# A gMLP and channel-MLP layer in fp32: the MLP's input moved by four transfers per block within SBUF, with its tokens held by fours

## The chip, the core and the metric

The kernel runs on one core of a Trainium2 chip. The metric is the device time of one execution, in microseconds (us), as the median of several runs. One further execution was recorded by the hardware profiler; all rows below come from it.

## What is computed

One layer over `x` of 1024 tokens by 1024 features, all in fp32. With `DEPTH` 1 only the first mixer, the gMLP, is used:

```python
hn = rms_norm(x, norm1_g)
z = gelu(hn @ w_in)                      # 1024 x 4096
u, v = split(z)
v = layernorm(v) * ln_g
sv = einsum('gts,bnsge->bntge', ws, v) + b_s      # causal ws, chunks of 128 tokens
x = x + (u * sv) @ w_out                 # 2048 -> 1024; the result is called y below
x = x + square(relu(rms_norm(x, norm2_g) @ w1)) @ w2   # 1024 -> 4096 -> 1024
return rms_norm(x, final_g)
```

## The kernel before

**Products.** The large matrix products are cut into products of 1024x1024 by 1024x1024, and each of these is done by a Strassen scheme: seven products of 512x512 blocks in place of eight. The code calls the left-hand blocks `a11`, `a12`, `a21`, `a22` and their sums `s1` to `s4`, the right-hand ones `b..` with sums `t..`, and the results `c11`, `c12`, `c21`, `c22`. Every fp32 operand is split into a high part (rounded to fp32r, ScalarE, ACT in the rows) and a low part (the rest, VectorE, DVE in the rows), and TensorE (PE) does three products for each: high by high, high by low, low by high (L438, L442, L443, function `products`).

**Stages.** A *single* (`single(n)`, n = 0 to 7) is one such 1024-deep product: n = 0, 1 make v, n = 2, 3 make u, n = 4 to 7 make the MLP's hidden layer. A *double* (`double(d)`) goes over 2048 of depth: d = 0 is the product with `w_out`, d = 1, 2 are those with `w2`. The order is singles 0 to 3, double 0, singles 4 to 7, doubles 1 and 2. Each has seven positions (`pos`), one per block product. A position has four units in a single and eight in a double, a unit being twelve matmuls of 128x512; below "unit (pos, k)" is the k-th of a position. The right operand of a unit is split into a ring of four entries (`ring_high`, `ring_low`; for doubles `pair_high`, `pair_low`, which hold both operands): ACT refills an entry when PE has left it (`split_high`, `split_pair_high`), DVE follows with the low part (`split_low`, `split_pair_low`), and PE waits for it before the unit (`low_done`). All engines run lists in program order, written out by hand; only semaphores join them. DVE also does the sums of the weights (`sum_t`), adds the finished banks of PSUM into `rows` (`add_rows` for doubles, `add_block` for singles), and SyncE (SP) issues nearly every transfer, on one queue.

**From double 0 to single 4.** y leaves double 0 in four blocks of 512 tokens by 512 features, held in `rows`, in the order c12, c22, c11, c21 (`Y_FINAL`: after positions 3, 4, 5, 6). Single 4 needs y transposed, as its left operand, so each block goes into a tile `quad_a..` by DMA, is turned by DVE's 32x32 transposes (`turn_y`, four instructions per block, into `raw_a..`), scaled by the norm's gain, and split. c12 becomes a11, c22 a21, c11 a12, c21 a22. Then come s3 from a21 and a11, s2 from a22 and s3 (`sum_turned`), s1 from s2 and a11 (`sum_combo`), and s4. Single 4 takes its left operands in the order a11 (pos 0), a12 (1), s2 (2), s1 (3), s3 (4), s4 (5), a22 (6).

How a block reaches its `quad` tile before the change:

- c12 and c22: SP stores the block to DRAM (`y_of`), waits for it to land, and loads it back by four transfers (`load_quads`, L808), one for each quarter of 32 partitions.
- c11: sixteen transfers within SBUF, all issued by SP (`move_quads`, L396), each of 32 partitions by 4 pieces of 512 bytes.
- c21: the same sixteen, eight issued by SP and eight by ACT.

Every block is also stored to DRAM, since double 1 needs y again as the residual (`load_rows`). The scheme holds token 128m + p on partition p of slice m; the reciprocal mean squares of y (`y_r2`), one per token, are computed at the start of double 1 and multiply PE's result in `add_rows`.

Of the kernel before, what the change touches and what calls it, by code (L numbers as in the profile page):

```python
# [10 lines left out]
P = 128  # L11
T = 1024
D = 1024
# [103 lines left out]
def trunk(nc, x, norm1_g, norm2_g, mlp_w1, mlp_w2, final_g, a_w_in, a_ln_g, a_ws, a_bs, a_w_out, out):  # L117
    x_v = x.rearrange("a (m p) d -> p (a m) d", p=P)
    out_v = out.rearrange("a (m p) d -> p (a m) d", p=P)
# [6 lines left out]
    with ExitStack() as ctx:  # L126
# [103 lines left out]
        y_r2 = tiny("y_r2", [P, MT])  # L230
        o_sq = tiny("o_sq", [P, 2, MT])
# [11 lines left out]
        scale_dram = nc.dram_tensor("row_scales", [MT, P], F32).ap()  # L243
        y_dram = nc.dram_tensor("y_blocks", [4, NB, NB], F32).ap()
# [6 lines left out]

        def y_of(blk):
            return y_dram[BLOCKS.index(blk)].rearrange("(k p) s -> p k s", p=P)

        def y_quadrant(blk, q):

            return y_dram[BLOCKS.index(blk)].rearrange("(t r) (q c) -> q r t c", r=32, q=4)[q]
# [78 lines left out]
        y_step = sem("y_step")  # L336
        o_squared = sem("o_squared")
# [299 lines left out]
        def _(sp):  # L637
# [87 lines left out]
            def single(n):  # L725
# [23 lines left out]
                if n in (3, 7):  # L749
                    filled(sp, ("product", n, 2), set_of(slot(n, 2))[3])  # L750
                    load_pair(0 if n == 3 else 1, "b11")
                if kind(n) == "v" or kind(n) == "hid":
# [30 lines left out]
                if kind(n) != "u":  # L783
                    store_block(n, "c22")
                if n not in (3, 7):
# [12 lines left out]
            def load_rows(d, blk):  # L798
# [3 lines left out]
                      "c22": x_v[:, 4:8, NB:]}[blk] if d == 0 else y_of(blk), rows_landed[blk], f"rows_{blk}")  # L802

            def load_quads(b, blk, dst):

                sp.wait_ge(y_stored[blk], 16)
                for q in range(4):
                    sp.dma_start(dst[32 * q:32 * q + 32, :, :], y_quadrant(blk, q)).then_inc(quads_landed[b], 16)  # L808

            def double(d):  # L810
# [90 lines left out]
                if d == 0:  # L901
                    y_final(sp, "c22")
# [1143 lines left out]
```

## Time and profile before

| | |
|---|---|
| median of 3 runs | 1123.8 us (1123.45 to 1123.99) |
| the profiled execution | 1123.38 us |
| its span | 1121.3 us |
| around the span | 2.1 us |
| PE busy | 1110.0 us, 99% |
| DVE busy | 796.9 us, 71% |
| ACT busy | 563.3 us, 50% |
| granted PE clock | 0.999 of full speed |
| DMA queue q1 | 49.6% of 16 engines, 194.28 MB |

The span goes from the first to the last record of the program. PE is busy nearly all of it, so what the kernel could still lose lies in PE's few gaps. Idle time of the other engines costs nothing unless PE waits for them.

### The profile page before, as it was taken

How to read it: one execution, taken by the hardware profiler on the slowest of the kernel's cores; microseconds unless marked ns; L12 is line 12 of the kernel's file. 1: busy time of each engine (PE TensorE's matmuls, PEld its weight loads, DVE VectorE, ACT ScalarE, POOL GpSimd, SP SyncE). 2: the span in 40 equal slices, each digit the busy share in tenths (PEclk: the TensorE clock that was granted, in tenths of full speed). 3: DMA queues.
4: the chain of work that ended last, by engine and by line, in shares of the span. 5: the costliest groups of instructions: out<-in, count | busy, mean ns of one | idle time of the engine just before them, and what ended most of it. 6: DMA issues, size and time to landing. Idle time of an engine off the chain costs nothing.

```text
span 1121.3 us, 13104 instructions
## 1 busy us (share of the span) xinstructions
PE 1110.0 (99%) x5050; PEld 922.8 (82%) x5050; DVE 796.9 (71%) x872; ACT 563.3 (50%) x870; POOL 23.0 (2%) x17
## 2 busy tenths in 40 slices
PE   9999999999999999999999999999999999999997
PEld 7888888888888888888788888888888888888886
DVE  5885656689779986699858447455598575677666
ACT  7764344554554434644674455454644333333456
POOL 0000000000000000000000000000000000000240
PEclk9999999999999999999999999999999999999999
DMA  9072353272875594643353635527878354343213
GB/s 333 16 222 106 107 181 109 93 256 81 319 256 196 186 351 153 191 122 103 114 187 144 194 113 191 196 102 272 301 292 298 121 217 188 113 151 113 78 73 150
DMA packets 86541, 195.90 MB, mean 175 GB/s; under 512 B 5048, under 2 KB 15312, under 8 KB 79824
## 3 DMA queue, kind: packets, MB, share of 16 engines
q1 hardware_dynamic: 85168, 194.28, 49.6%
q10 hardware_dynamic: 1312, 0.79, 0.3%
q8 instruction: 40, 0.66, 0.2%
q14 instruction: 21, 0.17, 0.0%
HBM read 134.23 MB, written 58.72 MB: 172 GB/s over the span
## 4 chain that ended last, share of the span: by engine, by line
PE 89%; DVE 7%; ACT 2%; issue 1%; DMA 1%; SPq 0%; DVEq 0%; ACTq 0%
PE banks L438 29%; PE banks L443 29%; PE banks L442 29%; PE banks L531 3%; DVE ring_low L1426 1%; DVE raw_a L1522 1%; DVE left_and_right L1462 1%; DMA left_and_right<-in_a_w_in_dram 1%; ACT ring_high L990 0%; DVE rows L1589 0%; DVE rows L1568 0%; ACT raw_a L1039 0%; DVE s_low L1512 0%; DVE raw_s L1555 0%; DVE pair_low L1434 0%
## 5 line engine op out<-in xcount | busy, mean ns | idle before, releaser
L1020 ACT ACTIVATE pair_high<-left_and_right 128x1024 fp32r<-128x1024 f32 x168 | 177.2, 1060 | 247.4 <-PE banks L438 199.5
L1426 DVE TENSOR_TENSOR ring_low<-left_and_right,ring_high 128x512 fp32r<-128x512 f32 x224 | 153.1, 693 | 186.0 <-ACT ring_high L990 185.3
L1434 DVE TENSOR_TENSOR pair_low<-left_and_right,pair_high 128x1024 fp32r<-128x1024 f32 x168 | 204.3, 1231 | 111.2 <-ACT pair_high L1020 111.2
L990 ACT ACTIVATE ring_high<-left_and_right 128x512 fp32r<-128x512 f32 x224 | 138.0, 628 | 254.6 <-PE banks L438 155.9
L438 PE MATMUL banks<-pair_high 128*128 128x512 f32 x672 | 262.0, 390 | 0.0
L442 PE MATMUL banks<-pair_low,pair_high 128*128 128x512 f32 x672 | 261.7, 389 | 0.0
L443 PE MATMUL banks<-pair_high,pair_low 128*128 128x512 f32 x672 | 261.7, 389 | 0.0
L438 PE MATMUL banks<-s_high,ring_high 128*128 128x512 f32 x384 | 150.0, 391 | 2.9 <-DVE s_low L1512 2.1
L442 PE MATMUL banks<-s_low,ring_high 128*128 128x512 f32 x384 | 149.6, 390 | 0.0
L443 PE MATMUL banks<-s_high,ring_low 128*128 128x512 f32 x384 | 149.5, 389 | 0.0
L438 PEld LDWEIGHTS banks<-pair_high 128*128 128x128 f32 x672 | 126.2, 188 | 26.4 <-DVE scratch L1616 0.3
L442 PEld LDWEIGHTS banks<-pair_low,pair_high 128*128 128x128 f32 x672 | 126.2, 188 | 26.2
L443 PEld LDWEIGHTS banks<-pair_high,pair_low 128*128 128x128 f32 x672 | 126.2, 188 | 26.0
L438 PE MATMUL banks<-a_high,ring_high 128*128 128x512 f32 x288 | 112.6, 391 | 0.0
L442 PE MATMUL banks<-a_low,ring_high 128*128 128x512 f32 x288 | 112.2, 390 | 0.0
L443 PE MATMUL banks<-a_high,ring_low 128*128 128x512 f32 x288 | 112.2, 389 | 0.0
L438 PEld LDWEIGHTS banks<-s_high,ring_high 128*128 128x128 f32 x384 | 72.1, 188 | 18.8 <-DVE s_low L1512 2.5
L443 PEld LDWEIGHTS banks<-s_high,ring_low 128*128 128x128 f32 x384 | 72.1, 188 | 14.9
L442 PEld LDWEIGHTS banks<-s_low,ring_high 128*128 128x128 f32 x384 | 72.1, 188 | 14.8
L1462 DVE TENSOR_TENSOR left_and_right<-left_and_right 128x2048 f32<-128x2048 f32 x32 | 73.2, 2288 | 1.0
L438 PEld LDWEIGHTS banks<-a_high,ring_high 128*128 128x128 f32 x288 | 54.1, 188 | 11.3 <-DVE scratch L1616 0.3
L443 PEld LDWEIGHTS banks<-a_high,ring_low 128*128 128x128 f32 x288 | 54.1, 188 | 11.2
(128 smaller groups left out, 1217.6 us busy)
## 6 DMA issues: line engine op xcount, KB each, us to landing
left_and_right<-sums SPq DMA_DIRECT2D x40, 1024.0 KB, 7.0
left_and_right<-in_mlp_w_dram SPq DMA_DIRECT2D x36, 1024.0 KB, 7.4
sums<-rows SPq DMA_DIRECT2D x34, 1024.0 KB, 5.3
left_and_right<-in_a_w_in_dram SPq DMA_DIRECT2D x19, 1024.0 KB, 7.3
v_blocks<-rows SPq DMA_DIRECT2D x8, 1024.0 KB, 4.5
left_and_right<-in_a_w_out_dram SPq DMA_DIRECT2D x8, 1024.0 KB, 10.0
rows<-in_x_dram SPq DMA_DIRECT2D x7, 1024.0 KB, 9.1
spare<-v_blocks SPq DMA_DIRECT2D x6, 1024.0 KB, 6.6
```

The costliest lines, as they stand in the source:

```text
L438: first = nc.tensor.matmul(ps[:, bank, :], stat_high, mov_high, start=start, stop=False, skip_group_check=True)
L442: nc.tensor.matmul(ps[:, bank, :], stat_high, mov_low, start=False, stop=False, skip_group_check=True)
L443: last = nc.tensor.matmul(ps[:, bank, :], stat_low, mov_high, start=False, stop=stop, skip_group_check=True)
L531: mm = nc.tensor.matmul(ps[:, banks[m], c * P:(c + 1) * P], held[:, c, m * P:(m + 1) * P], ws_t[:, g, :], start=True, stop=True)
L990: nc.scalar.activation(ring_high[k][:, :], right_place(n, pos)[:, k, :], ACT.Copy)\
L1020: nc.scalar.activation(pair_high[pair_entry(d, pos, k)][:, :, :], pair_of(d, pos, k), ACT.Copy)\
L1426: nc.vector.tensor_tensor(ring_low[k][:, :], right_place(n, pos)[:, k, :], ring_high[k][:, :].bitcast(F32), ALU.subtract).then_inc(low_don ...
L1434: nc.vector.tensor_tensor(pair_low[e][:, :, :], pair_of(d, pos, k), pair_high[e][:, :, :].bitcast(F32), ALU.subtract).then_inc(low_done, 1)
L1462: nc.vector.tensor_tensor(*args, ALU.subtract).then_inc(t_summed, 1)
L1522: nc.vector.transpose(dst[:, j, :], src[:, :, j:P:4]).then_inc(y_turned, 1)
```

## The change

**Transfers.** `move_quads` now issues four transfers for a block instead of sixteen: each takes all 128 partitions of one quarter of the features, and writes 32 partitions by 16 pieces of 512 bytes. All four blocks go this way, from SP alone; the way over DRAM is gone for c12 and c22, and ACT issues no transfer there. The store to DRAM follows behind the four transfers. For c22 the load of the last left block of double 0, `left(13)`, still stands ahead in SP's list.

**Token order.** Because of the new shape, column 128m + p of the transposed block is token 4p + m. The hidden layer and the result hold their tokens in that order; so the residual is loaded by `y_fours`, the output is written by a changed `out_v` (rows of 4 KB that lie 16 KB apart in DRAM, instead of side by side), and the scales `y_r2` must be rearranged: they are computed in single 6 (`scale_y`), stored to DRAM and loaded back as `y_r2_fours` in single 7, both by SP. DVE waits for that load before double 1's first `add_rows`.

**DVE's order.** The turns of a11 move up by a position, to between the splits for the start of position 5; the additions of c22 and c11 move to the end of the position before, ahead of the split of k = 3; the turns of a21 move from position 6 to the middle of position 5, those of a12 from the end to the middle of position 6, and a12's low parts to ahead of the first split of single 4. ACT's scaling of a11 and the high parts of a12 move likewise.

```diff
-        def move_quads(eng, b, blk, dst, quadrants):
-            for q in quadrants:
-                for r in range(4):
-                    eng.dma_start(dst[32 * q:32 * q + 32, r:4 * QT:4, :],
-                                  block_of[blk][32 * r:32 * r + 32, :, P * q:P * q + P]).then_inc(quads_landed[b], 16)
+        def move_quads(eng, b, blk, dst):
+            for q in range(4):
+                eng.dma_start(dst[32 * q:32 * q + 32, :, :], block_of[blk][:, :, P * q:P * q + P])\
+                  .then_inc(quads_landed[b], 16)
...
                 if d == 0:
                     y_final(sp, "c12")
+                    move_quads(sp, "a11", "c12", quad_a11)
                     sp.dma_start(y_of("c12"), block_of["c12"]).then_inc(y_stored["c12"], 16)
                 left(11)
-                if d == 0:
-                    load_quads("a11", "c12", quad_a11)
                 left(12)
...
                     y_final(sp, "c22")
+                    move_quads(sp, "a21", "c22", quad_a21)
                     sp.dma_start(y_of("c22"), block_of["c22"]).then_inc(y_stored["c22"], 16)
-                    load_quads("a21", "c22", quad_a21)
...
-                    move_quads(sp, "a22", "c21", quad_a22, (0, 1))
-                    sp.wait_ge(quads_landed["a22"], 256)
+                    move_quads(sp, "a22", "c21", quad_a22)
...
                 elif n == 4:
-                    high_turned("a12")
                     split_high(4, 1, 0)
-                    y_final(act, "c21")
-                    act.wait_ge(low_done, unit_double(0, 6, 7) + 1)
-                    move_quads(act, "a22", "c21", quad_a22, (2, 3))
                     split_high(4, 1, 1)
...
+                    early = d == 0 and pos > 4
+                    if not late and not early:
                         add_rows(d, pos - 1)
-                    if d == 0 and pos == 5:
-                        turn_y("a11")
-                    if d == 0 and pos == 6:
-                        turn_y("a21")
+                        low_a11(4, 0)
...
+                        if d == 0 and pos == 5 and k == 5:
+                            turn_y("a21", [0, 1])
+                        if d == 0 and pos == 5 and k == 6:
+                            turn_y("a21", [2, 3])
+                        if d == 0 and pos == 5 and k == 7:
+                            sum_turned("s3", [0, 1])
+                        if d == 0 and pos == 6 and k == 5:
+                            turn_y("a12", [0, 1])
+                        if d == 0 and pos == 6 and k == 6:
+                            turn_y("a12", [2, 3])
...
                     for k in range(4):
+                        if d == 0 and pos in (4, 5) and k == 3:
+                            add_rows(0, pos)
...
+                            if d == 0 and pos == 4:
+                                turn_y("a11", [k])
+                            if (d, pos, k) == (0, 5, 0):
+                                sum_turned("s3", [2, 3])
```

The order of DVE around the end of position 4 of double 0. `pair_low` is the low part of a unit's operands, `rows` the addition of a finished block of y, `raw_a11` and `raw_a21` are the turned blocks. Before, the split of unit (5, 3), then the additions and the turns of a11:

```order
L1434 TENSOR_TENSOR pair_low0_92<-left_and_right_77,pair_high0_87 128x1024
L1434 TENSOR_TENSOR pair_low1_93<-left_and_right_77,pair_high1_88 128x1024
L1589 TENSOR_TENSOR rows_78<-banks,rows_78 128x512 x4
L1522 STREAM_TRANSPOSE raw_a11_63<-quad_a11_71 128x512 x4
L1434 TENSOR_TENSOR pair_low2_94<-left_and_right_77,pair_high2_89 128x1024
L1434 TENSOR_TENSOR pair_low3_95<-left_and_right_77,pair_high3_90 128x1024
```

Now, from the split of unit (5, 2) on:

```order
L1437 TENSOR_TENSOR pair_low0_92<-left_and_right_77,pair_high0_87 128x1024
L1525 STREAM_TRANSPOSE raw_a11_63<-quad_a11_71 128x512
L1592 TENSOR_TENSOR rows_78<-banks,rows_78 128x512 x4
L1437 TENSOR_TENSOR pair_low1_93<-left_and_right_77,pair_high1_88 128x1024
L1525 STREAM_TRANSPOSE raw_a11_63<-quad_a11_71 128x512
L1437 TENSOR_TENSOR pair_low2_94<-left_and_right_77,pair_high2_89 128x1024
L1437 TENSOR_TENSOR pair_low3_95<-left_and_right_77,pair_high3_90 128x1024
L1525 STREAM_TRANSPOSE raw_a21_64<-quad_a21_72 128x512 x2
L1437 TENSOR_TENSOR pair_low0_92<-left_and_right_77,pair_high0_87 128x1024
L1525 STREAM_TRANSPOSE raw_a21_64<-quad_a21_72 128x512 x2
L1437 TENSOR_TENSOR pair_low1_93<-left_and_right_77,pair_high1_88 128x1024
```

A turn and the four additions have moved ahead of the split of unit (5, 3) (`pair_low1`), and the turns of a21 stand ahead of the splits of units (5, 6) and (5, 7), where none stood.

SP's list over the same stretch and on to single 4. Before:

```order
L887 DMA y_blocks<-rows_78 128x4x512
L644 DMA left_and_right_77<-sums 128x2048
L808 DMA quad_a11_71<-y_blocks 32x16x128 x4
L644 DMA left_and_right_77<-sums 128x2048 x2
L903 DMA y_blocks<-rows_78 128x4x512
L808 DMA quad_a21_72<-y_blocks 32x16x128 x4
L396 DMA quad_a12_73<-rows_78 32x4x128 x16
L908 DMA y_blocks<-rows_78 128x4x512
L644 DMA left_and_right_77<-in_mlp_w1_dram 128x4x512 x2
L396 DMA quad_a22_74<-rows_78 32x4x128 x8
```

Now:

```order
L398 DMA quad_a11_71<-rows_78 32x16x128 x4
L894 DMA y_blocks<-rows_78 128x4x512
L646 DMA left_and_right_77<-sums 128x2048 x3
L398 DMA quad_a21_72<-rows_78 32x16x128 x4
L909 DMA y_blocks<-rows_78 128x4x512
L398 DMA quad_a12_73<-rows_78 32x16x128 x4
L913 DMA y_blocks<-rows_78 128x4x512
L646 DMA left_and_right_77<-in_mlp_w1_dram 128x4x512 x2
L398 DMA quad_a22_74<-rows_78 32x16x128 x4
```

The two round trips over DRAM are gone, the third of the `sums` loads (`left(13)`) stays ahead of a21's move, and every block is moved by four transfers.

## Rows read from the trace of the kernel before

**Rows 1.** The page: busy us, share of the span, instructions.
```profile
PE 1110.0 (99%) x5050; PEld 922.8 (82%) x5050; DVE 796.9 (71%) x872; ACT 563.3 (50%) x870; POOL 23.0 (2%) x17
```

**Rows 2.** Waits of PE, 440:600: waited for, us in total, times, longest.
```profile
PE banks L438 <- DVE s_low L1512: 2.1, 1, 2.1
PE banks L438 <- DVE ring_low L1426: 0.7, 2, 0.4
```

**Rows 3.** Timeline of PE: start us, us, engine line, operands, [idle before <-releaser].
```profile
458.65 0.39 PE L438 MATMUL banks<-pair_high 128*128 128x512 f32 x1
...
502.17 0.39 PE L438 MATMUL banks<-a_high,ring_high 128*128 128x512 f32 x1
...
523.93 0.39 PE L438 MATMUL banks<-s_high,ring_high 128*128 128x512 f32 x1
...
538.35 0.50 PE L438 MATMUL banks<-s_high,ring_high 128*128 128x512 f32 x1 [2.12 <-DVE s_low L1512]
...
541.20 0.39 PE L438 MATMUL banks<-s_high,ring_high 128*128 128x512 f32 x1
```

**Rows 4.** Timeline of DVE, from the end of position 4 to single 4.
```profile
460.02 1.22 DVE L1434 TENSOR_TENSOR pair_low<-left_and_right,pair_high 128x1024 fp32r<-128x1024 f32 x1 [1.27 <-ACT pair_high L1020]
461.17 2.48 DVE L1589 TENSOR_TENSOR rows<-banks,rows 128x512 f32<-128x512 f32 x4
463.56 4.05 DVE L1522 STREAM_TRANSPOSE raw_a<-quad_a 128x512 f32<-128x512 f32 x4
...
507.50 2.75 DVE L1500 SCALAR_TENSOR_TENSOR a_low<-raw_a,g_fours,a_high 128x512 fp32r<-128x512 f32 x4
...
513.58 1.10 DVE L1522 STREAM_TRANSPOSE raw_a<-quad_a 128x512 f32<-128x512 f32 x1
...
536.00 2.29 DVE L1512 TENSOR_TENSOR s_low<-raw_s,s_high 128x2048 fp32r<-128x2048 f32 x1
```

**Rows 5.** DVE in 440:565 by shape: count, busy us, mean ns, idle before.
```profile
L1434 DVE TENSOR_TENSOR pair_low<-left_and_right,pair_high 128x1024 fp32r<-128x1024 f32 x20 | 23.9, 1217 | 11.6 <-ACT pair_high L1020 11.6
L1426 DVE TENSOR_TENSOR ring_low<-left_and_right,ring_high 128x512 fp32r<-128x512 f32 x25 | 16.9, 688 | 6.8 <-ACT ring_high L990 6.6
L1522 DVE STREAM_TRANSPOSE raw_a<-quad_a 128x512 f32<-128x512 f32 x16 | 16.7, 1076 | 0.0
L1555 DVE SCALAR_TENSOR_TENSOR raw_s<-raw_a,neg_g,raw_a 128x512 f32<-128x512 f32 x4 | 2.8, 746 | 0.0
```

**Rows 6.** Timeline of the queues of SP and ACT; the time is that of issuing.
```profile
461.27 0.34 SPq L644 DMA_DIRECT2D left_and_right<-sums  x1
463.74 0.37 SPq L903 DMA_DIRECT2D y_blocks<-rows  x1
468.75 1.91 SPq L808 DMA_DIRECT2D quad_a<-y_blocks  x4
485.49 10.42 SPq L396 DMA_DIRECT2D quad_a<-rows  x16
...
506.58 5.50 ACTq L396 DMA_DIRECT2D quad_a<-rows  x8
```

**Rows 7.** DMA by issue: KB each, median us from issue to landing.
```profile
left_and_right<-sums SPq DMA_DIRECT2D x1, 1024.0 KB, 4.8
...
quad_a<-rows SPq DMA_DIRECT2D x16, 64.0 KB, 2.0
```

**Rows 8.** Busy time by stretch; the last two: share of 16 DMA engines, GB/s.
```profile
466.00:468.00 2.00, 2.00 (x11) 1.65 (x10) 2.00 (x3) 1.86 (x4) 0.00 (x0) 1.00 1.03 402
470.00:474.00 4.00, 4.00 (x19) 3.34 (x18) 0.98 (x1) 4.00 (x12) 0.00 (x0) 1.00 1.09 230
471.00:474.00 3.00, 3.00 (x15) 2.50 (x14) 0.00 (x0) 3.00 (x10) 0.00 (x0) 1.00 1.13 209
508.00:513.00 5.00, 5.00 (x23) 4.14 (x23) 5.00 (x7) 0.80 (x2) 0.00 (x0) 1.00 0.88 200
```

**Rows 9.** Tile row_scales: from issue to landing of the scales' two transfers.
```profile
DMA to landing us min/median/max: 9.4/11.6/13.8
```

More of the change, by code:

```diff
@@ L801, in load_rows @@
                      {"c11": x_v[:, 0:4, 0:NB], "c12": x_v[:, 0:4, NB:], "c21": x_v[:, 4:8, 0:NB],
[L802 to L808, printed above, removed]
+                      "c22": x_v[:, 4:8, NB:]}[blk] if d == 0 else y_fours(blk), rows_landed[blk], f"rows_{blk}")
             def double(d):
@@ L902, in double @@
                     y_final(sp, "c22")
+                    move_quads(sp, "a21", "c22", quad_a21)
                     sp.dma_start(y_of("c22"), block_of["c22"]).then_inc(y_stored["c22"], 16)
-                    load_quads("a21", "c22", quad_a21)
                     sp.wait_ge(low_done, unit_double(0, 5, 7) + 1)
                     y_final(sp, "c11")
-                    move_quads(sp, "a12", "c11", quad_a12, range(4))
+                    move_quads(sp, "a12", "c11", quad_a12)
                     sp.dma_start(y_of("c11"), block_of["c11"]).then_inc(y_stored["c11"], 16)
@@ L1305, in double @@
                         square_rows(2, "c11", o_sq, o_squared, (0, 1))
+                    if pos == 5 and d == 0:
+                        scale_a11()
                     split_pair_high(d, pos, 5)
+                    if pos == 5 and d == 0:
+                        high_a11()
                     if pos == 6 and d == 2:
@@ L1312, in double @@
                         square_rows(d, "c12", y_sq if d == 0 else o_sq, y_squared if d == 0 else o_squared)
+                    split_pair_high(d, pos, 6)
+                    if pos == 5 and d == 2:
+                        square_rows(2, "c22", o_sq, o_squared)
+                    split_pair_high(d, pos, 7)
                     if pos == 5 and d == 0:
-                        scale_a11()
-                    split_pair_high(d, pos, 6)
-                    if pos == 5 and d == 0:
-                        high_a11()
-                    if pos == 5 and d != 1:
-                        square_rows(d, "c22", y_sq if d == 0 else o_sq, y_squared if d == 0 else o_squared)
-                    split_pair_high(d, pos, 7)
+                        square_rows(0, "c22", y_sq, y_squared)
                     if pos == 6 and d == 0:
                         square_rows(0, "c11", y_sq, y_squared)
+                        high_turned("a12")
                     for k in range(4):
@@ L1384, in _ @@
             act.wait_ge(o_done_b, MT)
-            act.dma_start(out_v[:, 7, NB:], rows[:, 7, NB:]).then_inc(last_stored, 16)
+            act.dma_start(out_v[1, :, 3, NB:], rows[:, 7, NB:]).then_inc(last_stored, 16)
         @block.vector
@@ L1518, in turn_y @@
                             "a22": (quad_a22, raw_a22)}[blk]
-                dve.wait_ge(quads_landed[blk], 64 if blk in ("a11", "a21") else 256)
+                dve.wait_ge(quads_landed[blk], 64)
                 dve.wait_ge(low_done, unit_double(0, 3 if blk == "a12" else 4, 7) + 1)
@@ L1695, in single @@
                 elif n == 4:
-                    low_turned("a12")
                     split_low(4, 1, 0)
@@ L1699, in single @@
                     split_low(4, 1, 1)
-                    for k in range(2):
-                        turn_y("a22", [k])
-                        sum_turned("s2", [k])
+                    turn_y("a22", [0])
+                    sum_turned("s2", [0])
                     split_low(4, 1, 2)
+                    turn_y("a22", [1])
+                    sum_turned("s2", [1])
                     split_low(4, 1, 3)
```

60 lines of the change are left out of this document (37 added, 23 removed).

## The prediction

> **What bounds the kernel now.** The page comes first: PE is busy 99% of the span [rows 1]. It does the same matmuls before and after, so the change can give back only gaps of PE. The waits of PE come next: in the stretch around the turn from double 0 to single 4 there are three, 2.1 us on a low part of a sum (L1512) and 0.7 us in two pieces on the ring's low parts [rows 2]. The timeline of PE gives what they cost in all. Units follow one another every 2.72 us: the first of position 5 starts at 458.65 and the first of single 4, sixteen units later, at 502.17 [rows 3]. From 523.93 (single 4, position 2) to 541.20 are five units, which should take 13.6 us and take 17.27. So 3.67 us are lost, idle time and slow restarts together, and that is **all that this change can win**: 0.33% of the time.
>
> Why PE waits there is to be seen on DVE. Its chain runs without a break from the first turn of a22, at 513.58, to the end of s1's low part, 536.00 + 2.29 = 538.29 [rows 4]: 24.7 us of work in a fixed order, and PE starts on s1 (position 3) at 538.35 [rows 3]. Without stalls PE would be due there at 502.17 + 12 x 2.72 = 534.8. So s1 is in time if a22's first turn starts by about 510.0, less the 0.1 us or so from DVE's end to PE's start. It starts at 513.58 because the block's sixteen transfers take that long: ACT is busy issuing its eight for 5.50 us from 506.58 on, SP with the other eight beside it [rows 6].
>
> **The price on which all hangs: S, the time for one block (1 MiB) as four transfers.** The trace has no such transfer. Nearest is the load of c22's quads from DRAM, with the same four destinations of 32 partitions and the same 512-byte pieces: it moves 230 GB/s over 470 to 474 and 209 over 471 to 474, the engines' share being above 1 [rows 8]. 1.049 MB at these rates takes 4.6 and 5.0 us. The old moves within SBUF go at 200 GB/s at a share of 0.88, held back by their issue [rows 8]: 5.2 us, my upper end by rows. The lower end is the store of a block in 2 KB pieces over all partitions, 402 GB/s [rows 8]: 2.6 us. I take **S = 4.8**, since the pieces and the destination are those of the quads' load; the source differs (SBUF, not DRAM). To this comes the way to the first packet and the landing of the last: a 64 KB move lands 2.0 us after its issue [rows 7], 0.3 of it its own bytes, so a whole block alone lands 1.7 + S = 6.5 us after the first issue.
>
> The Trainium skill (SBUF — State Buffer, Door 1: The DMA port swizzle) speaks against a fast move: partitions 0 to 31, or any 32 that start at a multiple of 32, reach only 8 of 16 ports, about 218 GB/s, so a transfer that writes one quarter of the partitions is held to half the rate. By that S would be 4.8, where the bare 402 GB/s of the store would make it 2.6. The rates of the quads' load, 209 to 230 GB/s, agree with it, although they come from DRAM.
>
> **Part 1, a11 (c12).** The move starts at once instead of after a store and its landing. a11's turns go into DVE's gaps: 11.6 us of idle time stand before the 20 splits in this stretch [rows 5]. Worth nothing by itself, since PE does not wait here. The load of `left(11)` comes behind 1 MiB more of moves, some 5 us later; it is first read for unit (5, 4), due at 469.5, and issued near 445.
>
> **Part 2, a21 (c22): a new wait.** Before, the split of (5, 3) ends at 460.02 + 1.22 = 461.2, and SP issues `left(13)` at 461.27, since that load waits for it [rows 4, 6]. Now a turn and four additions stand ahead: the split of (5, 2) ends at 458.75, then 1.0 for the turn, 2.4 for the additions and 1.1 for the split (the steps of these groups in rows 4 and 5, where back-to-back instructions overlap by 0.09), so 463.3 (458.75 is 460.02 less the idle 1.27). `left(13)` goes out 2.0 us later, and a21's move queues behind it on the same queue. The load lands 4.8 us after its issue [rows 7]; its packets free the queue some 0.7 earlier, at 463.3 + 4.05 = 467.35. Then S, then 0.35 to land: **472.5**. DVE has come to the turns of a21 some 5 us earlier and stands there, with the split of (5, 6) queued behind two turns. That split ends at 472.5 + 2.0 + 1.2 = 475.7; PE is due on (5, 6) at 458.65 + 6 x 2.72 = 474.97 [rows 3] and starts 0.15 after DVE's end: **0.9 us of stall**. The next unit costs DVE two turns and a split, 3.1 us, against PE's 2.72: **0.4** more.
>
> **Part 3, a12 (c11).** From 472.5 DVE is full: four turns (4.0), five splits of pairs (5.7), four pieces of s3 (2.6) and the four additions (2.4), 14.8 in all with their joins [rows 4, 5]. c11 is final at 487.3, its move lands at 487.3 + 1.7 + 4.8 = 493.8. Meanwhile DVE does 5.1 us of other work and idles a little. From 493.8 come four turns (4.0), two pair splits (2.3), a12's low parts (2.6), two ring splits (1.2) and the additions of c21 (2.4): c21 is final at **506.3**. Single 4's first unit is due at 502.17 plus the 1.3 already lost and its first ring split ends at 503.4: **0.1**.
>
> **Part 4, a22 (c21).** Its move lands at 506.3 + 6.5 = **512.8**, only 0.7 us sooner than before, though ACT no longer issues. The 24.7 us chain then ends at 537.6. PE, by now 1.4 us later and with some 0.2 us of slow restarts, is due on s1 at 534.8 + 1.6 = 536.4 and starts at 537.8: **1.4 us**. The two small waits on the ring go, as PE's lateness covers them.
>
> **Part 5, the rest, at nothing.** The scales' two transfers land in 9.4 and 13.8 us by the like of single 0 [rows 9]; the second is issued in position 6 of single 7, and double 1's first additions come after a whole position of eight units, 22 us, so DVE's wait finds it landed. The output's rows of 4 KB now lie 16 KB apart; the pieces are as long as before, and I bound this by 0.3 us either way. ACT's moved work has gaps around it.
>
> **Sum.** Stalls after: 0.9 + 0.4 + 0.1 + 1.4 = 2.8, and 0.25 for restarts, 3.1 against 3.67 now. The gain is 0.6 us: 1123.4 - 0.6 = 1122.8 for an execution like the profiled one, which lies 0.4 under the median of 1123.8. So **1123.2 us**. As the three moves a21, a12, a22 stand one behind the other, with DVE full between them, each 0.1 us in S is 0.3 in the time. S of 4.56 gives 1122.4, 5.24 gives 1124.5.
>
> **The rivals.** 2.25 us (0.2%) is about what a measurement can tell from no change.
>
> *All stalls gone.* SBUF as source gives the engines shorter packets than DRAM, and S is at most 4.2. Then a21's turns start by 471.9, PE loses 0.7 there at the most, and s1 is in time. For it: the store's 402 GB/s shows that the engines can do more, and the engines' share of 0.88 at 200 GB/s leaves room for 227 [rows 8]. Against it: the share above 1 at 209 GB/s, which looks like a limit at the destination. Time: 1120.3 to 1121.5, or 1120.1 at best.
>
> *The moves are slow and the stalls grow.* One mechanism: each transfer reads 128 partitions and writes 32, all sixteen engines crowd on the same 32, and S is 5.75 or more. From there the time is over 2.25 us worse. At S = 6 the first stall is 2.1, splits (6, 6) and (6, 7) stall by 0.8, (4, 0, 0) by 0.5, and all three old waits are back with 3.1: with restarts 6.9 against 3.67, 1127.0 us. For it: a new shape that nothing in the trace shows, and DVE blocked in order behind each landing. Against it: the same destination pattern at 4.6 to 5.0.
>
> *The change does nothing for a22.* If c21's move were bound by issue as before, it would land where it did, and the new stalls at (5, 6) would be pure loss, hidden in part by s1's old wait: 1123.5 to 1124.5, the same for a measurement. It is in my middle case.
>
> **How the numbers follow.** The middle case, S from 4.3 to 5.7, has 0.60, and its own range is 1121.6 to 1125.5. All stalls gone has 0.26, slow moves 0.14. The range reaches down to the best case, 1120.1, and up to S of 5.6 with the 0.3 us of the output, 1125.9. Faster by over 0.2%: 0.26; within: 0.60; slower: 0.14.
>
> **What would show it.** In the changed kernel's timeline of DVE the first turn of a21 should start near 472.5, that of a12 near 493.8, of a22 near 512.8, each after an idle time ended by a DMA; PE should show new waits on `pair_low` in position 5, about 1.3 us together, and one on `s_low` of about 1.2. The rate over 468 to 472 should be 210 to 230 GB/s. If it is above 250, or the turns of a21 start before 471.9, the middle case is wrong towards faster; if the rate is below 185, towards slower. A wait of DVE for the scales, or a gap in PE anywhere outside 470 to 540, would mean that I missed something.

## The result, and the profile after

The change makes the kernel slower. Four runs of the changed kernel have a median of 1139.9 us (1139.1 to 1140.6), the kernel before beside them 1123.9. The ratio is 1.0143, with a 95% interval of 1.0124 to 1.0163. Forecast were 1123.2 us and a range up to 1125.9, so the time lies 14 us above the range. (One run of the kernel before took 1396 us in a disturbed execution; the ratio leaves it out.)

The page's first part, where [rows 1] stood:

```profile
span 1138.7 us, 13083 instructions
PE 1115.4 (98%) x5050; PEld 924.4 (81%) x5050; DVE 796.8 (70%) x872; ACT 564.0 (50%) x870; POOL 23.0 (2%) x17
```

The span is 17.4 us longer, with as many matmuls and the same work on DVE and ACT. PE's own busy time is 5.4 us longer, although it does the same matmuls; the granted clock below accounts for most of that. The waits of PE and of DVE over 440 to 600, against [rows 2]:

```profile
PE banks L440 <- DVE pair_low L1437: 9.3, 2, 7.0
PE banks L440 <- DVE ring_low L1429: 2.6, 4, 0.7
PE banks L440 <- DVE s_low L1515: 2.1, 1, 2.1
```

```profile
DVE raw_a L1525 <- DMA quad_a<-rows: 24.6, 3, 11.3
```

The wait on the sum's low part is as long as before. New is a wait on the pairs' low parts, 7.0 us at once, and above it DVE's: three times, 24.6 us in all, it stands before the turns of a block until the block's transfers have landed. Each is seen in the timelines of SP, with the issue of the moves, and of DVE, with the turns (the transposes of `raw_a`; in brackets the idle time before):

```profile
463.32 3.10 SPq L398 DMA_DIRECT2D quad_a<-rows  x4
...
493.28 2.71 SPq L398 DMA_DIRECT2D quad_a<-rows  x4
...
517.75 2.77 SPq L398 DMA_DIRECT2D quad_a<-rows  x4
```

```profile
478.45 2.04 DVE L1525 STREAM_TRANSPOSE raw_a<-quad_a 128x512 f32<-128x512 f32 x2 [11.31 <-DMA quad_a<-rows]
...
505.09 2.05 DVE L1525 STREAM_TRANSPOSE raw_a<-quad_a 128x512 f32<-128x512 f32 x2 [6.09 <-DMA quad_a<-rows]
...
529.40 1.09 DVE L1525 STREAM_TRANSPOSE raw_a<-quad_a 128x512 f32<-128x512 f32 x1 [7.20 <-DMA quad_a<-rows]
```

From a block's first issue to its first turn it takes 11.8 us for a12 (493.28 to 505.09) and 11.65 for a22 (517.75 to 529.40); for a21 it takes 15.1, since `left(13)` goes ahead of it. The prediction had 6.5. The stretches of time say the same as a rate; the columns are start and end, length, busy time of PE, PEld, DVE, ACT and POOL, then TensorE's granted clock, the share of the DMA engines and GB/s:

```profile
470.00:474.00 4.00, 4.00 (x19) 3.34 (x18) 0.00 (x0) 4.00 (x10) 0.00 (x0) 1.00 1.27 119
474.00:478.00 4.00, 0.67 (x3) 0.21 (x2) 0.00 (x0) 0.32 (x1) 0.00 (x0) 1.00 1.16 199
478.00:482.00 4.00, 0.34 (x1) 0.34 (x2) 3.55 (x4) 0.00 (x0) 0.00 (x0) 0.70 0.34 130
482.00:486.00 4.00, 4.00 (x10) 3.12 (x10) 4.00 (x6) 1.06 (x1) 0.00 (x0) 0.50 0.00 0
```

From 470 to 474 only the moves are under way (the store of the block, in its 2 KB pieces, comes behind them and lifts the next stretch): 119 GB/s, with the engines' share at 1.27, where the quads' load had 230 [rows 8]. So the DMA engines are not idle; it is their packets that take long.

The last column but two, the granted clock, tells most of PE's longer busy time. After the pause of 7 us the clock is granted at 0.50 (1.2 GHz), and from the second start on PE's timeline shows steps of 0.43 us instead of 0.23:

```profile
474.28 0.39 PE L445 MATMUL banks<-pair_high,pair_low 128*128 128x512 f32 x1
481.66 0.79 PE L440 MATMUL banks<-pair_high 128*128 128x512 f32 x1 [6.99 <-DVE pair_low L1437]
482.25 0.63 PE L444 MATMUL banks<-pair_low,pair_high 128*128 128x512 f32 x1
482.68 0.63 PE L445 MATMUL banks<-pair_high,pair_low 128*128 128x512 f32 x1
```

Adding up each gap between two starts beyond 0.227 us over 440 to 584 gives 3.6 us for the kernel before and 21.2 for the changed one. The difference, 17.6, is the 17.4 of the span to within 0.2. 2.3 us are slow steps after the first pause, 1.6 slow steps after the wait for s1 at 551.6; the rest is waiting.

### The profile page after: what moved, and what is told of

Same layout as the page of the kernel before. It is cut to its first block, busy times and chain, and to the rows that moved or that the text cites. A ratio compares the mean times of both kernels' runs of the same rounds, so it can differ in the third digit from the quotient of the medians.

```text
span 1138.7 us, 13083 instructions
## 1 busy us (share of the span) xinstructions
PE 1115.4 (98%) x5050; PEld 924.4 (81%) x5050; DVE 796.8 (70%) x872; ACT 564.0 (50%) x870; POOL 23.0 (2%) x17
## 4 chain that ended last, share of the span: by engine, by line
PE 86%; DVE 6%; DMA 3%; issue 2%; ACT 2%; SPq 1%; DVEq 0%; POOL 0%; ACTq 0%; POOLq 0%
PE banks L440 28%; PE banks L445 28%; PE banks L444 28%; DMA quad_a<-rows 3%; PE banks L533 3%; DVE ring_low L1429 1%; DVE raw_a L1525 1%; DVE left_and_right L1465 1%; DVE pair_low L1437 1%; DVE rows L1592 1%; SPq L398 1%; ACT ring_high L994 0%; DVE raw_s L1558 0%; DVE rows L1571 0%; DVE s_low L1515 0%
## 5 line engine op out<-in xcount | busy, mean ns | idle before, releaser
L440 PEld LDWEIGHTS banks<-pair_high 128*128 128x128 f32 x672 | 126.7, 188 | 37.2 <-DVE pair_low L1437 10.7
L445 PEld LDWEIGHTS banks<-s_high,ring_low 128*128 128x128 f32 x384 | 72.4, 188 | 15.1
```

Source lines behind the costliest of these rows:

```text
L440: first = nc.tensor.matmul(ps[:, bank, :], stat_high, mov_high, start=start, stop=False, skip_group_check=True)
L445: last = nc.tensor.matmul(ps[:, bank, :], stat_low, mov_high, start=False, stop=stop, skip_group_check=True)
```

## Is it the time of the moves? Sixteen transfers again, on one queue and on two

Two theories stood against each other. *Time of the move*: DVE's order puts three moves in series, and each is some 5 us longer than forecast. *Order*: the new order of DVE costs the 16 us, whatever the transfers take. Both runs keep DVE's order and the token order of the change, and move each block in sixteen pieces of 64 KB to the same places. Each piece reads every fourth partition, 32 in all, so size and number of partitions read change together here; the measurements further below take them apart.

```diff
             for q in range(4):
-                eng.dma_start(dst[32 * q:32 * q + 32, :, :], block_of[blk][:, :, P * q:P * q + P])\
-                  .then_inc(quads_landed[b], 16)
+                for r in range(4):
+                    eng.dma_start(dst[32 * q:32 * q + 32, 4 * r:4 * r + 4, :],
+                                  block_of[blk][r:P:4, :, P * q:P * q + P]).then_inc(quads_landed[b], 16)
```

On SP alone:

> The change as it is, but each block moved by sixteen transfers of 64 KB (32 partitions to 32) from SyncE's queue alone, to the same places. Before, sixteen such took 10.42 us to issue and landed 2.0 us after their issue, so a block takes 12.4 us from the first issue, against 2.8 + 8.3 = 11.1 with the four transfers. Theory time of the move (the three moves in series, nothing else): 1.3 us more in each of three, 1139.9 + 3.9 = 1143.8. Theory order (VectorE's new order costs the 16 us, whatever the transfers take): 1139 to 1141.

Measured: 1139.06 us (1137.9 to 1139.9), ratio 1.0127 (1.0110 to 1.0144). That is the number of the *order* theory, and the expectation of the other one missed by 4.7 us. The trace tells why. The first turns wait for a DMA here as well:

```profile
476.20 2.04 DVE L1526 STREAM_TRANSPOSE raw_a<-quad_a 128x512 f32<-128x512 f32 x2 [8.74 <-DMA quad_a<-rows]
502.96 2.04 DVE L1526 STREAM_TRANSPOSE raw_a<-quad_a 128x512 f32<-128x512 f32 x2 [6.20 <-DMA quad_a<-rows]
528.38 1.08 DVE L1526 STREAM_TRANSPOSE raw_a<-quad_a 128x512 f32<-128x512 f32 x1 [8.32 <-DMA quad_a<-rows]
```

a21 is turned 2.2 us earlier than with the four, since the sixteen are issued while `left(13)` is still under way, which hides a part of their issue. a12's move then takes 11.9 us from its first issue (491.04) and a22's 12.8 (515.59), 0.1 and 1.1 more than the four. The three together make 1.0 us, and the time is 0.8 us shorter than the changed kernel's. Three equal losses were wrongly expected, and this run by itself does not tell the theories apart.

With half of the transfers of a21, a12 and a22 issued by ACT:

```diff
-                    move_quads(sp, "a21", "c22", quad_a21)
+                    move_quads(sp, "a21", "c22", quad_a21, (0, 1))
+                    sp.wait_ge(quads_landed["a21"], 256)
...
                     if pos == 5 and d == 0:
+                        y_final(act, "c22")
+                        move_quads(act, "a21", "c22", quad_a21, (2, 3))
                         scale_a11()
```

> As the one before, but eight of the sixteen transfers of the last three blocks are issued by ScalarE, at the places where it has just split a half. 5.2 to 5.5 us of issue and 2.0 us to land give about 7.4 us from the first issue, where the prediction had taken 6.5 and the changed kernel takes 11.1. Theory time of the move: 3.7 us less in each of three, 1139.9 - 11.1 = 1128.8, or 1123.2 + 3 x 0.9 = 1125.9 counted from the prediction; so 1125 to 1130. Theory order: stays at 1138 to 1141.

Measured: 1127.09 us (1126.0 to 1130.1), ratio 1.0020 (1.0010 to 1.0030) against a kernel before that had 1125.5 beside it. That lies in the 1125 to 1130 of *time of the move*. Over 12 us are gone without a touch on DVE's order, which the *order* theory can't have. The turns of a21 start at 472.94, and those of a12 wait for no transfer:

```profile
472.94 2.11 DVE L1538 STREAM_TRANSPOSE raw_a<-quad_a 128x512 f32<-128x512 f32 x2 [0.48 <-DMA quad_a<-rows]
...
495.67 2.09 DVE L1538 STREAM_TRANSPOSE raw_a<-quad_a 128x512 f32<-128x512 f32 x2
...
517.34 1.10 DVE L1538 STREAM_TRANSPOSE raw_a<-quad_a 128x512 f32<-128x512 f32 x1 [0.26 <-DMA quad_a<-rows]
```

472.94 is what was forecast for the four transfers (472.5), and still this kernel is no faster than the one before. One reason is the price of ACT's help. Eight issues hold it for 5.7 us, the scaling of a11 and the next split stand behind them, and DVE's split of the next unit, ahead of the turns, waits 6.22 us for it (the last row). The other reason is PE's wait on s1, which is as long as before; more of it below.

```profile
461.89 5.69 ACTq L399 DMA_DIRECT2D quad_a<-rows  x8
467.69 2.56 ACT L1061 ACTIVATE raw_a<-raw_a,g_fours 128x512 f32<-128x512 f32 x4 [5.10 <-issue]
...
471.23 1.23 DVE L1450 TENSOR_TENSOR pair_low<-left_and_right,pair_high 128x1024 fp32r<-128x1024 f32 x1 [6.22 <-ACT pair_high L1028]
```

## Are the moves in series? One block alone, and the old order

First, of the changed kernel a21's move alone goes by sixteen transfers over the two queues, with a12 and a22 as they are.

> The change as it is, but c22's move into a21 alone by sixteen transfers of 64 KB, eight each on SyncE's and ScalarE's queue, as in the run with all three; a12 and a22 by four. There a21's first turn began at 472.9, with the change at 478.5. Theory series: 5.5 us less, 1139.9 - 5.5 = 1134.4, and the first turns of a12 and a22 come 5.5 earlier as a whole. Theory that the last move alone sets the end (a22 is what s1 waits for): unchanged near 1139.

Measured: 1134.06 us (1133.0 to 1134.7), ratio 1.0079 (1.0062 to 1.0095). The first turns of the three blocks:

```profile
473.69 2.10 DVE L1535 STREAM_TRANSPOSE raw_a<-quad_a 128x512 f32<-128x512 f32 x2 [1.01 <-DMA quad_a<-rows]
...
499.79 2.04 DVE L1535 STREAM_TRANSPOSE raw_a<-quad_a 128x512 f32<-128x512 f32 x2 [5.50 <-DMA quad_a<-rows]
...
524.02 1.08 DVE L1535 STREAM_TRANSPOSE raw_a<-quad_a 128x512 f32<-128x512 f32 x1 [6.68 <-DMA quad_a<-rows]
```

They come 4.8, 5.3 and 5.4 us earlier than in the changed kernel, and the time falls by 5.8, where 5.5 were expected. What one move saves is handed on whole through the two others. They are in series.

Then the reverse: all four moves by four transfers, with the new token order and the scales over DRAM, but DVE's and ACT's order as it was before the change (of its diff only a part is shown).

```diff
-                        if d == 0 and pos == 5 and k == 5:
-                            turn_y("a21", [0, 1])
-                        if d == 0 and pos == 5 and k == 6:
-                            turn_y("a21", [2, 3])
...
+                    if d == 0 and pos == 5:
+                        turn_y("a11")
+                    if d == 0 and pos == 6:
+                        turn_y("a21")
```

> The change's four transfers for all four blocks, with the tokens by fours and the scales through HBM, but VectorE's and ScalarE's order as before: a11 and a21 turned late, ahead of positions 5 and 6 of the double, a12's low parts in single 4. Only two moves are then waited for at once. a12: 485.5 + 11.7 = 497.2, before its turns of 498.8, so nothing. a22: 506.6 + 11.65 = 518.2 where the first turn started at 513.6, so 4.6 us. Theory series (the loss is the move's time, as often as VectorE's order waits for it): 1123.8 + 4.6 = 1128.4, that is 11.5 less than with the new order, because a21's and a12's moves have slack again. Theory moves alone (the slow transfers cost the same under any order): 1137 or more. Theory order alone (the new order costs the 16 us): 1123.5 to 1124.5.

Measured: 1129.16 us (1127.8 to 1129.8), ratio 1.0036 (1.0024 to 1.0048) with 1124.4 for the kernel before beside it, so 4.8 us over it by the medians and 4.0 by the ratio, where 4.6 were expected. Of all the turns only the first of a22 waits; the turns of a12, the first row, do not:

```profile
498.69 2.09 DVE L1523 STREAM_TRANSPOSE raw_a<-quad_a 128x512 f32<-128x512 f32 x2
...
518.07 1.08 DVE L1523 STREAM_TRANSPOSE raw_a<-quad_a 128x512 f32<-128x512 f32 x1 [4.49 <-DMA quad_a<-rows]
```

The same slow transfers cost 4 to 5 us under the old order and 16 under the new one. The old order turns a21 some 20 us after its block is final and so does not feel that move. In this trace the gaps of PE over 440 to 584 add up to 9.7 us, 6.1 more than before, and the span is 6.1 us longer: nothing is left for the token order, the scales and the output's rows. (3.1 of the 9.7 are slow steps at 1.2 GHz after the pauses at 518 and 540; not every execution need have them, and the medians differ by less.)

## What makes a block slow: the transfers by themselves

Four kernels compute nothing, but move one block of 1 MiB in one form after the other, with no engine at work beside it.

> Nothing of the reference is computed; the output is x read back. One block of 1 MiB lies in SBUF as in the kernel (128 partitions, 4 x 512 elements in each) and is moved by fourteen forms, one after the other, each landed before the next is issued. In the changed kernel a block's four transfers (each reads 128 partitions and writes 32) land one every 2.27 us. Theory shape (a transfer that reads 128 partitions and writes only 32 within SBUF is slow by itself): here too about 2.3 us for each of the four, 9 us a block; straight to the same partitions in pieces of 512 bytes well below, 5 us or less; 32 partitions to 32 others in the same pieces under 5 us; 128 to 32 in pieces of 2 KB as slow as in 512 bytes. Theory load (the transfers are slow because three engines and TensorE use SBUF at the same time): all forms near 5 us here. Theory pieces (a move within SBUF in pieces of 512 bytes costs about 80 ns a piece in any shape): every form with 512-byte pieces near 9 us, the one with 2 KB pieces near 5, and from HBM to the same places 5. The sixteen transfers of 64 KB are held up by their issue, 10.4 us, in every theory.

What SyncE waited for after the last issue of a form (in all, times, longest):

```profile
SPq L55 <- DMA four_fourths<-rows: 8.6, 1, 8.6
SPq L55 <- DMA wide_pieces<-rows: 7.6, 1, 7.6
...
SPq L55 <- DMA from_dram<-blocks: 4.6, 1, 4.6
...
SPq L55 <- DMA straight<-rows: 2.7, 1, 2.7
```

With the 2.7 us of issue the four transfers of the change (`four_fourths`) take 11.3 us here too. So it is not the load of the other engines. It is not the piece either: in 2 KB pieces (`wide_pieces`) it is 10.2 with the issue. From HBM to the same 32 partitions it is 7.2, within SBUF to the same 128 partitions 5.4. The sixteen transfers of 64 KB on one queue take 11.7 and 11.9 us, 10.3 and 10.4 of them issue.

> Nothing of the reference is computed; the output is x read back. As in the first measurement a block of 1 MiB is moved by one form after the other, nothing else running; this time the number of partitions read and written is varied, all in pieces of 512 bytes that do not merge. Known: 128 to 32 lands 11.3 us after its first issue (packets of 82 ns), HBM to 32 in 7.2 (38 ns), 32 to 128 in 8.0 (39 ns), 128 to the same 128 in 5.4 (28 ns). Theory both sides (a transfer within SBUF is held by the narrower side, and writing 32 partitions while reading costs twice): 32 to 32, of the same partitions or others, as slow as 128 to 32, 11 us. Theory spread (slow is that each DMA engine reads eight partitions and writes two, the ratio of read to written partitions being four): 128 to 64 and 64 to 32 in between, 8 to 9 us, 64 to 64 and 32 to 32 near 6 to 7.5 us. Theory queue (a transfer alone takes 47 ns a packet, queued behind others 82): two, landed, then two takes 2 x (0.65 + 1.7 + 4.5) = 13 us or less and its packets are at 50 to 60 ns. Over two queues, the sixteen of 64 KB should land 7.4 us after the first issue, the eight of 128 KB from 64 partitions in 2.7 + 2.3 = 5 to 6 us if their packets are fast.

The rates while each form ran (the last number), of the second measurement; in order: 128 partitions to 32, 64 to 32, 64 to 64, 128 to 64, 32 to 32:

```profile
16.00:24.00 8.00, 0.00 (x0) 1.00 1.25 105
40.00:47.00 7.00, 0.00 (x0) 1.00 1.06 141
50.00:55.00 5.00, 0.00 (x0) 1.00 0.90 209
57.00:65.00 8.00, 0.00 (x0) 1.00 1.22 131
68.00:72.00 4.00, 0.00 (x0) 1.00 0.95 221
```

Equal numbers of partitions go at 209 to 221 GB/s (192 where 32 are moved onto themselves), fewer written than read at 105 to 141. The same form of four, 128 to 32, moved 125, 105 and 117 GB/s in the first three measurements, so differences of this size between forms mean little. *Both sides* falls with 32 to 32 being fast, and *queue* explains a part at most: two, landed, then two took 13.6 us, not 13 or less. *Spread* put 128 to 64 at 8 to 9 us, and it took 10.7 (55.72 to 66.47) against the 11.8 of 128 to 32. Over two queues the eight of 128 KB, 64 to 32, moved 166 GB/s and took 9.1 us where 5 to 6 were expected, the sixteen of 64 KB, 32 to 32, 7.7. It looked like a rule on partitions, so the next set tried to break it.

> Nothing of the reference is computed; the output is x read back. Third set of forms, nothing else running. So far the packets of 512 bytes took 82 to 85 ns for 128 partitions to 32, 76 for 128 to 64, 61 for 64 to 32, but 28 for 128 to the same 128, 35 for 64 to 64, 35 to 38 for 32 to 32, 39 for 32 to 128 and 38 for HBM to 32. Theory fewer written than read (what is slow is a transfer within SBUF that writes fewer partitions than it reads): sixteen of 64 KB with 128 partitions to 32 (one m each) clearly above the 27 to 34 ns of sixteen of 64 KB with 32 to 32; 32 to 16 at 60 or more, HBM to 16 well below that. Theory size (it is the 256 KB transfers queued one behind the other that are slow, whatever their shape): the sixteen of 64 KB near 30 ns also with 128 to 32. Four to the same 32 partitions, and 1 MiB in one transfer to 32 partitions: near 82 ns in both, since each of the four already writes only one quarter at a time.

The sixteen of 64 KB, each from 128 partitions to 32, showed packets of 27 ns: the contrary of what *fewer written than read* expected. But they moved only 102 GB/s, held by their issue, so they never came to the rate at which the others are slow. The rest of the set: eight of 128 KB that read every second partition move 141 GB/s, as 64 neighbours to 32 did; four times to the same 32 partitions 122; 1 MiB in one transfer to 32 partitions 106. 32 to 16 moves 116, but HBM to 16 moves only 124, so there the 16 partitions alone are a limit and the pair tells nothing.

> Nothing of the reference is computed; the output is x read back. Sixteen transfers of 64 KB on one queue move only 105 GB/s, less than the 117 to 125 GB/s of the four of 256 KB, so their 27 ns a packet could not tell shape from size. Here the sixteen are issued over two queues, eight each, which offers some 200 GB/s. Theory shape (within SBUF, 128 partitions to 32 goes at about 120 GB/s in transfers of any size): the sixteen with 128 partitions to 32 take about 10 us from first issue to landing, packets of 50 ns and more, while the sixteen with 32 to 32 take 7.4 as before, at 27 to 30 ns. Theory size (transfers of 256 KB in a row are slow, those of 64 KB are not): both take 7.4 us. The four of 256 KB over two queues: 10.4 us as before.

The rates of the fourth measurement: sixteen of 64 KB over two queues with 128 partitions to 32, the same with 32 to 32, sixteen on one queue, four of 256 KB over two queues:

```profile
15.00:20.00 5.00, 0.00 (x0) 1.00 0.81 199
23.00:28.00 5.00, 0.00 (x0) 1.00 0.71 198
31.00:40.00 9.00, 0.00 (x0) 1.00 0.35 102
42.00:49.00 7.00, 0.00 (x0) 1.00 1.19 134
```

The same 128 partitions to 32 that go at 105 to 134 GB/s in transfers of 256 KB go at 199 in pieces of 64 KB, and the block lands 7.8 us after its first issue (13.69 to 21.48) instead of 10.3 to 11.8. That speaks for *size* and against *shape*, and yet it is not size alone: 256 KB from 32 partitions to 32 went at 221. Of the forms tried, slow are those that have both, a transfer of 128 KB or more within SBUF and fewer partitions written than read. With the size the number of pieces changed too: a transfer of 64 KB reads one piece of each partition and writes four to each, one of 256 KB reads four and writes sixteen. No form holds one and varies the other, so which of the two it is, and which accesses meet in such a transfer, stays open.

## The old 3.6 us: the sums in steps

Every kernel so far keeps PE's wait of 2.1 us on s1's low part. PE's timeline shows what fixes it: the start of a unit of position 2 that waits for the ring's low part, and the start on s1. First the kernel before (its start on s1, 538.35, is in [rows 3]), then the one with two queues, then the changed one:

```profile
529.84 0.47 PE L438 MATMUL banks<-s_high,ring_high 128*128 128x512 f32 x1 [0.31 <-DVE ring_low L1426]
...
533.82 0.47 PE L441 MATMUL banks<-s_high,ring_high 128*128 128x512 f32 x1 [0.71 <-DVE ring_low L1442]
...
542.33 0.50 PE L441 MATMUL banks<-s_high,ring_high 128*128 128x512 f32 x1 [2.12 <-DVE s_low L1528]
...
545.64 0.47 PE L440 MATMUL banks<-s_high,ring_high 128*128 128x512 f32 x1 [0.71 <-DVE ring_low L1429]
...
554.15 0.50 PE L440 MATMUL banks<-s_high,ring_high 128*128 128x512 f32 x1 [2.12 <-DVE s_low L1515]
```

It is 8.51 us from the one to the other in all three. The ring's split belongs to the same chain of DVE that goes on to s1, so once PE has waited for it, the wait on s1 is set by DVE's work in between. That does not show that an earlier a22 would not help: in every run its first turn came later than the 513.58 of the kernel before. What can be tested is the other way, to shorten the chain. In DVE's order four additions (2.4 us) and one whole low part (2.3 us) stand right ahead of PE's start on s1. This run takes the kernel before, leaves its moves alone, and makes s1's and s3's low parts in four steps. It also moves some splits of the ring ahead, on ACT those for position 2 ahead of s2's last two high parts (of the diff only DVE's part for s1 is shown):

```diff
-STEPPED = {0: ["a11", "s2"], 4: ["a11", "a12", "s2", "a22"]}
+STEPPED = {0: ["a11", "s2"], 4: ["a11", "a12", "s2", "s1", "s3", "a22"]}
...
-                add_block(n, "c11")
-                split_low(n, 3, 0)
+                if n == 4:
+                    add_block(4, "c11", (0, 1))
+                    split_low(4, 3, 0)
+                    low_step(4, "s1", 0)
+                    add_block(4, "c11", (2, 3))
+                    low_step(4, "s1", 1)
```

> The kernel before, its moves as they are; only in single 4 the low parts of s1 and s3 are made in four steps each instead of one (s1's first step and the ring's split ahead of the last two additions), and ScalarE splits the ring for position 2 ahead of s2's last two high parts. No move is touched. Before, TensorE loses 3.62 us in this stretch: 0.54 and 0.67 on the ring, 2.39 on s1's low part, with 0.6 x 4 us of additions and 2.3 us of one whole low part ahead of it. Theory chain (all that could be won lies in VectorE's order behind a22, not in the moves): all of it goes, 1123.9 - 3.6 = 1120.3, by 0.3%. Theory move (the 3.6 us hang on when c21's block lands): the wait only goes on to the next sum, s3's low part two positions later, 1123 to 1124.

Measured: 1120.24 us (1119.9 to 1121.4), ratio 0.9959 (0.9945 to 0.9972). It beats both kernels; the kernel before had 1125.4 beside it. PE's waits over 440 to 600 are down to one:

```profile
PE banks L438 <- DVE ring_low L1437: 0.9, 1, 0.9
```

In the two traces the gaps of PE fall from 3.62 us to 1.15, and the span from 1121.3 to 1118.9: 2.5 us, of the 3.6 that *theory chain* had counted; that its 1120.3 was met so closely is in part luck. The steps and the moved splits were not tried apart. The ring's split for position 1 now comes 0.9 us late, behind two turns. The medians differ by more, 3.6 us against the kernel before in its first session and 5.2 beside it. A clock that falls after s1's wait in some executions of the kernel before would do that (those with the lowest mean clock, 0.997, are among the longest), but none of them was profiled.

The same steps under the new order with two queues:

> The new order with the sixteen transfers over two queues (measured 1.002 of the kernel before, some 2.3 us over it), with the steps of the run before this one. In the two-queue kernel TensorE lost 7.6 us: 3.3 before 506 us on the splits that wait for a21's and a12's moves and for ScalarE, 4.3 after it on the ring and on s1's low part. Theory chain: the 4.3 go, 1126.2 - 4.3 = 1121.9 to 1122.5, above the kernel before with the same steps by the 3.3 us less the cover that TensorE's lateness gives later, so 1 to 2 us. Theory move: 1125 to 1127.

Measured: 1124.1 us (1123.6 to 1125.3), ratio 0.9990 (0.9981 to 0.9999), 1.6 us above what was expected for it at most; the steps gave 3.0 of the 4.3 us. In its trace PE loses 3.6 us, all of it before 506.4: on splits behind the turns of a21 and a12, and on splits that DVE could make only when ACT was done issuing (DVE waits 6.20 us for ACT ahead of a21's turns and 2.15 ahead of a12's). With s1's wait gone this is the price of the new order and of ACT's help together, 2.5 us more than the old order with the same steps; the two were not taken apart. Of the 3.9 us between the two medians the rest is elsewhere; in the profiled execution the last output write landed after 3.6 us instead of 2.4.

## Why the prediction was wrong, point by point

**What bounds the kernel** held: some 3.6 us could be won, and the run with the steps won 2.5 of them in its trace, but from DVE's and ACT's order and not from the moves. "s1 is in time if a22's first turn starts by about 510.0" was reached by no run and is not shown; the run with the steps has s1 in time with a22's first turn at 514.88. That the chain runs "without a break" was misread: twice DVE waits there for ACT's half of a ring entry.

```profile
525.31 0.69 DVE L1426 TENSOR_TENSOR ring_low<-left_and_right,ring_high 128x512 fp32r<-128x512 f32 x1 [0.62 <-ACT ring_high L990]
```

The chain is as long as it was taken, from 513.58 to 538.29, but 1.2 us of it are waits, and the run with the steps has none of them between a22's third turn and s1.

**The step that failed is the price S, "the time for one block (1 MiB) as four transfers".** Taken: 4.8 us, between 2.6 and 5.24. By the way the prediction counts, it was 10.1 for a12 (505.09 - 493.28 - 1.7), 9.95 for a22 and 10.75 for a21, and 9.6 with nothing beside it. The value came from the load from HBM, which has another source, the upper end from moves of 64 KB, which also read only 32 partitions each, and the lower end from the store, which goes to HBM in larger pieces. None of them is a transfer of 256 KB within SBUF from 128 partitions to 32, and that form lay outside them all. "The source differs (SBUF, not DRAM)" was written down as a remark and given no price. In the measurements it is worth the whole factor, 208 GB/s from HBM against 105 to 125; the smaller transfers win back nearly as much, 199.

**The rule of the skill** that was weighed there, the Trainium skill, SBUF — State Buffer, Door 1: The DMA port swizzle (8 of 16 ports for any 32 partitions, about 218 GB/s), agrees within some 5% where it was to apply: HBM to 32 partitions moved 208 GB/s, and 64 to 64 no more than 32 to 32 (209 and 221). At best it is a bound from above, and the four transfers of the change reached only 105 to 125. Agreement with rows of another source was no evidence for this one.

**Part 1** held: a11 costs nothing. **Part 2**: `left(13)` and the move were issued at the forecast time (462.83 and 463.32, for 463.3), the turns came at 478.45 for 472.5. **Part 3**: c11 final at 493.28 for 487.3, a12's turns at 505.09 for 493.8. **Part 4**: a22's turns at 529.40 for 512.8, s1 at 554.15 for 537.8. The lateness grows by 6.0, 5.3 and 5.3 us: three times the same term. One more step of Part 4 failed, though S hides it: the two small waits on the ring were to go, and s1's to shrink to 1.4. In the run with two queues, whose a21 was turned at 472.94, ring waits of 0.7 and 0.4 stayed and s1's was 2.1. **Part 5** held: from PE's last matmul to the end of the span it is 6.4 us before and after, and DVE has no wait for the scales.

**The slope** held. "Each 0.1 us in S is 0.3 in the time", 1122.4 at 4.56 and 1124.5 at 5.24, is 3.1 per microsecond; at S = 10.1 that gives 1123.2 + 3.1 x 5.3 = 1139.6, and 1139.9 was measured. That it is so close is in part luck. The slope counts S alone, and s1 was 16.35 us late by it; the 1.6 us of slow steps behind s1 come on top in the profiled execution, and that one lies 0.65 above the median. The slow steps at 482 to 486 cost little in the end: at 508.30 PE had to wait for DVE again, 2.35 us.

**The rival** "the moves are slow and the stalls grow" named the mechanism, 128 read and 32 written, and was given 0.14. Its price was worked out at S = 6, with no reason why a form that no row shows should stop there. What was said would tell against the forecast, a rate below 185 GB/s, did: 119.

## What to carry to other kernels

When the trace has no transfer of the new form, rows that share one property with it each are not two ends of a range: measure the form alone, or let the range reach to a multiple. Before a transfer is put on the path, count how often the order waits for such a one in series, for its error comes back as often; here a threefold slope turned 5 us into 16. And ask first whether the stall can be taken out of the chain behind the transfer instead: sums in steps and splits moved ahead won 0.4% with no transfer touched.

## What the runs showed of the hardware

- Within SBUF, transfers of 256 KB that read 128 partitions and write 32 or 64 moved 105 to 134 GB/s; 64 KB pieces of the same form, issued from two queues, 199; 256 KB with as many partitions written as read 192 to 221; HBM to 32 partitions 208.
- With nothing beside it a block of four transfers landed 11.1 to 11.8 us after its first issue (10.3 over two queues), one of sixteen after 11.7 to 11.9 on one queue and after 7.6 to 7.8 on two. Merging sixteen into four saved 7.6 us of SyncE's issue time on one queue, and next to nothing until the block had landed.
- PE came back from a pause of 7 us at a granted clock of 0.50 and ran some eleven matmuls at 0.43 us each. After s1's wait of 2.1 us it did so in the changed kernel (0.59 over 554 to 558), but not after the same wait in the kernel before (1.00 over 538 to 542). How much PE had idled before does not sort these cases: with sixteen transfers on SP alone PE had lost more before s1's wait than with the old order and the new moves, and yet the clock stayed at 1.00 behind it (554 to 558), where with the old order it fell (0.57 over 543 to 547).
